# Weights fetched ahead in a handed-on area, gate stores on ScalarE's queue, and bfloat16 one-hots in pairs of tokens

## The reference

```python
mix = concat([mo * head_norm(mlstm), silu(rg) * head_norm(retention)])
x = x + mix @ w_out
hn = rmsnorm(x, rms_ffn_g)
# peer_ffn(hn): 8 heads, 128 x 128 experts, the best 16 for each token and head
q = hn @ w_query
s = einsum('thpd,hpkd->thpk', q, sub_keys)            # two halves p, 128 keys each
s1, i1 = top_k(s[:, :, 0], 16);  s2, i2 = top_k(s[:, :, 1], 16)
top_s, top_pos = top_k(s1[..., :, None] + s2[..., None, :], 16)   # over the 256 pairs
e_idx = (i1 * 128 + i2) at top_pos;  gate = softmax(top_s)
a = gelu(einsum('thkd,td->thk', peer_u[e_idx], hn))
x = x + einsum('thk,thkd->td', gate * a, peer_v[e_idx])
y = rmsnorm(x, rms_final_g)
```

## Time and profile before

| | us |
|---|---|
| median of 3 runs (3445.17 to 3450.38) | 3448.93 |
| the profiled execution | 3455.61 |
| its span | 3453.8 |
| load of a `wq`, 1 MB, from issue to landing (median) | 5.3 |
| store of a sub-block of the gate, 4 MB, from issue to landing (median) | 14.0 |
| mean granted clock of TensorE over the span, as a share of full speed | 0.969 |

### The profile page before, as it was taken

One profiled execution on the slowest core, in us unless ns is written; L12 is line 12 of the kernel. 1 busy time (PEld: TensorE's weight loads), 2 busy tenths in 40 slices (PEclk: granted clock), 3 DMA queues, 4 the chain that ended last, 5 costly groups with the idle time before them and its releaser, 6 DMA issues. The chain is left out here.

```text
span 3453.8 us, 49287 instructions
## 1 busy us (share of the span) xinstructions
PE 3288.0 (95%) x17444; PEld 2899.8 (84%) x17444; DVE 2489.7 (72%) x4965; ACT 991.0 (29%) x1479; POOL 737.1 (21%) x565
## 2 busy tenths in 40 slices
PE   7999999697999899999899999997999999999998
PEld 5766777486999899999899999986888888888886
DVE  5565545433999869999757777755888888988884
ACT  3212322221111123444322222222333334333332
POOL 0000000000000000000056656644333333433320
PEclk9999999798999999999999999998999999999999
DMA  2111110222111123556699999978999999999982
GB/s 103 38 38 50 52 49 26 74 80 86 68 68 68 54 86 114 180 180 209 193 349 373 373 364 359 362 296 311 403 367 352 353 353 371 380 369 352 354 318 110
DMA packets 323282, 749.94 MB, mean 217 GB/s; under 512 B 22312, under 2 KB 153772, under 8 KB 322016
## 3 DMA queue, kind: packets, MB, share of 16 engines
q1 hardware_dynamic: 243392, 458.51, 37.2%
q0 software_dynamic: 79776, 290.00, 22.3%
HBM read 633.48 MB, written 114.95 MB: 217 GB/s over the span
## 5 line engine op out<-in xcount | busy, mean ns | idle before, releaser
L1083 PE MATMUL u_p<-hn_hi,u_hi 128*128 128x384 f32 x2048 | 701.6, 343 | 35.9 <-PEq L1437 16.2
L1084 PE MATMUL u_p<-hn_lo,u_hi 128*128 128x384 f32 x2048 | 695.0, 339 | 0.0
L1085 PE MATMUL u_p<-hn_hi,u_lo 128*128 128x384 f32 x2048 | 694.8, 339 | 0.0
L1552 POOL DMA_INDIRECT s_ring<-in_peer_u,row_idx x264 | 332.1, 1258 | 1298.4 <-DVE row_idx L1642 1075.0
L1797 PE MATMUL y_p<-v_hi,w_hi 128*128 128x512 f32 x1536 | 474.5, 390 | 18.6 <-DVE w_lo L1882 17.0
L1754 POOL DMA_INDIRECT y_ring<-in_peer_v,row_idx x240 | 356.9, 1487 | 622.2 <-DVE yt L1891 555.9
L1802 PE MATMUL y_p<-v_hi,w_lo 128*128 128x512 f32 x1536 | 473.7, 390 | 0.0
L1799 PE MATMUL y_p<-v_lo,w_hi 128*128 128x512 f32 x1536 | 473.7, 390 | 0.0
L1823 ACT ACTIVATE v_hi<-v_raw 128x1024 fp32r<-128x1024 f32 x256 | 257.2, 1052 | 666.5 <-PE y_p L1802 654.5
L1878 DVE TENSOR_TENSOR v_lo<-v_raw,v_hi 128x1024 fp32r<-128x1024 f32 x256 | 302.1, 1221 | 171.1 <-ACT v_hi L1823 154.9
L1083 PEld LDWEIGHTS u_p<-hn_hi,u_hi 128*128 128x128 f32 x2048 | 387.9, 189 | 38.2 <-issue 24.8
(11 more groups left out here) (312 smaller groups left out, 4621.9 us busy)
## 6 DMA issues: line engine op xcount, KB each, us to landing
v_raw<-in_peer_v SPq DMA_DIRECT2D x128, 1024.0 KB
u_raw<-in_peer_ut SPq DMA_DIRECT2D x128, 512.0 KB
act_scratch<-act_tile SPq DMA_DIRECT2D x128, 384.0 KB
gate_scratch<-gbuf SPq DMA_DIRECT2D x12, 4096.0 KB, 14.0
a_raw<-act_scratch SPq DMA_DIRECT2D x128, 384.0 KB
g_raw<-gate_scratch SPq DMA_DIRECT2D x128, 384.0 KB, 8.7
wp_raw<-in_w_heads SPq DMA_DIRECT2D x64, 256.0 KB, 3.4
wq<-in_w_query SPq DMA_DIRECT2D x8, 1024.0 KB, 5.3
```

Source lines behind the costliest of these rows:

```text
L1083: mm(b, uh[:, s, k, :], hn_hi[:, k, t], start=(k == 0), stop=False)
L1084: mm(b, uh[:, s, k, :], hn_lo[:, k, t], start=False, stop=False)
L1085: last = mm(b, ul[:, s, k, :], hn_hi[:, k, t], start=False, stop=(k == ND - 1))
L1552: nc.gpsimd.indirect_dma_start(out=ring[:, s, :], out_offset=None, in_=src, in_offset=bass.IndirectOffsetOnAxis(ap=idx[:, column:column + ...
```

## The change

An area `late` of 32 KB a partition lives through the whole kernel and is handed from stage to stage: weights `wp_hi` and `wp_lo` of the heads, low parts of `w_out`, first query weights (raw, high, low) and `sub_keys`, work arrays of decode, second buffer of `gbuf`, `s_hb`, and two of the four slots of the down phase. With it:

1. `w_out` is loaded by SP after the last projection of the heads, all eight blocks at once, into the place of `xn_lo` (which is therefore in two parts, written by two operations). Five blocks are rounded within the block of the heads, the other three at the start of the output projection, and `out` takes the blocks in the order `WO`.
2. The first query weights and `sub_keys` are loaded after the last output product and rounded at the end of that block. The block that cleared semaphores is gone; GpSimd clears them in the blocks that follow.
3. The gate's store is issued on ScalarE's queue at the end of each sub-block, and the block's end waits for the first buffer only; GpSimd waits for the second ahead of the first load into `s_hb`.
4. The one-hots are bfloat16, with the two tokens of a pair innermost. The gate is split at the end of decode into three bfloat16 parts (`gp`), the keys are copied (`eb`), and a step has five VectorE operations (`one2` = second key, `raw` = first key, and `raw` times each gate part into `one1`) and 24 bfloat16 matmuls, which sum the three parts in PSUM; each reads one token of the pairs, every second element.
5. The first two slots of the down phase are loaded in the block before it, after the last dot product; the waits for the stores of the gelus move behind the other two loads.

The core of the diff, shortened:

```diff
+SLOT = 2 * D + 4 * TL * P
+class Query:                       # views into the area "late"
+        self.raw = late[:, 0:2048]...;  self.hi, self.lo = late_r[...] for n in (1, 2)
+        self.keys = late[:, 6144:8192]...
+class Pair:                        # one slot of the down phase: v, a, g in SLOT columns
+    def load(self, sp, A, a_dram, g_dram, g, j):    # the three loads of the old load()
+        late_r, late = twin(top, "late", [P, NK * SUB])
...
 mixer_stages, block of the heads:
+    wh, wl = (late[:, n * 4096:(n + 1) * 4096].rearrange("p (k d) -> p k d", k=ND) for n in range(2))
+    xla, wo_a = twin(own, "xn_lo_a", [P, 3, T]);   xlb, wo_b = twin(st, "xn_lo_b", [P, 5, T])
+WO = [3, 4, 5, 6, 7, 0, 1, 2]
+    def wo_high(act, j, wo_b=None):
+        raw, hi, lo = wo_parts(WO[j], wo_b)             # raw in xn_lo's place, hi in xn_hi's, lo in late
+        act.wait_ge(*wo_in[j])
+        nc.scalar.activation(hi, raw, ACT.Copy, scale=gnm[:, WO[j]:WO[j] + 1]).then_inc(wohi_done, 1)
+    def wo_low(dve, j, wo_b=None):
+        raw, hi, lo = wo_parts(WO[j], wo_b)
+        dve.wait_ge(wohi_done, j + 1)
+        nc.vector.scalar_tensor_tensor(lo, raw, gnm[:, WO[j]:WO[j] + 1], hi.bitcast(F32), ALU.mult,
+                                       ALU.subtract).then_inc(wolo_done, 1)
+            sp.wait_ge(S["pj_done"], NTILE)
+            for j, k in enumerate(WO):
+                sp.dma_start(wo_parts(k, wo_b)[0], A["w_out"][:, k, :]).then_inc(wo_in[j][0], 16)
...
+            for j in range(5):                          # ScalarE
+                wo_high(act, j, wo_b)
             head_root(NH - 1)
...
-                v.tensor_tensor(xl[:, :, s], pb..., xh[:, :, s].bitcast(F32), ALU.subtract).then_inc(S["lo"], 1)
+                v.tensor_tensor(xla[:, :, s], pk[:, 0:3, 0:r], xh[:, 0:3, s].bitcast(F32), ALU.subtract)
+                v.tensor_tensor(xlb[:, :, s], pk[:, 3:ND, 0:r], xh[:, 3:ND, s].bitcast(F32),
+                                ALU.subtract).then_inc(S["lo"], 1)
+                    if n == NTILE - 1:                  # VectorE
+                        wo_low(dve, 0, wo_b)
...
+            wo_low(dve, 1, wo_b)
             finish(NH - 1)
+            for j in range(2, 5):
+                wo_low(dve, j, wo_b)
 block of the output projection:
+            for s in old[0]:                            # GpSimd; expire() returns the old semaphores
+                pool.sem_clear(s)
-            for k in range(2):
-                sp.dma_start(wo[:, k, :], A["w_out"][:, k, :]).then_inc(wo_in[k], 16)
-            for k in range(2, ND):
-                sp.wait_ge(wolo_done, k - 1)
-                sp.dma_start(wo[:, k % 2, :], A["w_out"][:, k, :]).then_inc(wo_in[k % 2], 16)
+                if t == NT - 2:
+                    sp.wait_ge(y_done, 2 * NT)
+                    sp.dma_start(first_query.raw, A["w_query"][0]).then_inc(first_query.wq_in, 16)
+                    sp.dma_start(first_query.keys, A["sub_keys"]).then_inc(first_query.sk_in, 16)
-                    for k in range(ND):
+                    for j, k in enumerate(WO):
                         if u == 0:
-                            pe.wait_ge(wolo_done, k + 1)
+                            pe.wait_ge(wolo_done, j + 1)
+            act.wait_ge(first_query.wq_in, 16)
+            ac(first_query.hi, first_query.raw, ACT.Copy).then_inc(first_query.hi_done, 1)
             h_high(NT - 1)
...
             h_low(NT - 1)
+            dve.wait_ge(first_query.hi_done, 1)
+            v.tensor_tensor(first_query.lo, first_query.raw, first_query.hi.bitcast(F32), ALU.subtract)
 end of decode (VectorE):
+                dve.wait_ge(t_out, PET)
+                ch.mark(v.tensor_copy(e3s[:, :, :], e3T[:, :, DENSE:DENSE + NS]))
+                ch.mark(v.tensor_copy(eb[:, :, :], e3T[:, 0:2, 0:DENSE]))
+                ch.link(v.tensor_copy(gp[:, 0, :], e3T[:, 2, 0:DENSE]))
+                ch.link(v.tensor_tensor(left[:, :], e3T[:, 2, 0:DENSE], gp[:, 0, :], ALU.subtract))
+                ch.link(v.tensor_copy(gp[:, 1, :], left[:, :]))
+                ch.link(v.tensor_tensor(left[:, :], left[:, :], gp[:, 1, :], ALU.subtract))
+                ch.link(v.tensor_copy(gp[:, 2, :], left[:, :]))
 gate block:
+        one1 = sb(st, "one1", [P, 2, 3, TWO, NK, 2], BF16)
+        one2 = sb(st, "one2", [P, 2, TWO, NK, 2], BF16)
+        raw = sb(st, "raw", [P, TWO, NK, 2], BF16)
-                    sp.wait_ge(bank_out, (2 * NSTEP) * (2 * j + s + 1) + 4)
-                    sp.dma_start(g_dram[...], gbuf[:, s, ...]).then_inc(saved[s], 16)
-            for s in range(2):
-                sp.wait_ge(saved[s], 16 * (NSUB // 2) + 16)
+            sp.wait_ge(saved[0], 16 * (NSUB // 2) + 16)
-                            last = nc.tensor.matmul(pg[...], one2[:, b, k, :], one1[:, b, k, :], start=True, stop=True)
+                            for q in range(3):
+                                last = nc.tensor.matmul(pg[...], one2[:, b, k // 2, :, k % 2],
+                                                        one1[:, b, q, k // 2, :, k % 2], start=(q == 0), stop=(q == 2))
+                    act.wait_ge(bank_out, (2 * NSTEP) * (2 * j + s + 1) + 4)        # end of a sub-block
+                    nc.scalar.dma_start(g_dram[...], gbuf[s]...).then_inc(saved[s], 16)
-                        v.tensor_tensor(raw[:, :, :], io, col[1], ALU.is_equal).then_inc(raw_done, 1)
-                        v.tensor_tensor(one1[:, b], io, col[0], ALU.is_equal).then_inc(hot1, 1)
+                        v.tensor_tensor(one2[:, b], key, e2, ALU.is_equal).then_inc(hot2, 1)
+                        dve.wait_ge(hot1, 3 * i + 1)
+                        v.tensor_tensor(raw[:, :, :, :], key, e1, ALU.is_equal).then_inc(raw_done, 1)
                         dve.wait_ge(raw_done, i + 1)
-                        v.tensor_tensor(one2[:, b], raw[:, :, :], col[2], ALU.mult).then_inc(hot2, 1)
+                        for q in range(3):
+                            part = gp[:, q, t].rearrange(...).unsqueeze(2).broadcast_to(two)
+                            v.tensor_tensor(one1[:, b, q], raw[:, :, :, :], part, ALU.mult).then_inc(hot1, 1)
 block of the gathers:
+                if n == 15:                             # GpSimd
+                    pool.wait_ge(saved[1], 16 * (NSUB // 2) + 16)
+            sp.wait_ge(dot_done, NU)
+            for s in range(2):
+                Pair(sem, s, late[:, s * SLOT:(s + 1) * SLOT]).load(sp, A, a_dram, g_dram, 0, s)
             for p in range(2):
                 a_store(sp, NK - 2 + p, p)
-            for p in range(2):
-                sp.wait_ge(a_out[p], 16 * (NK // 2))
 down phase:
-            for s in range(SLOTS):
-                load(sp, 0, s, s)
+            for s in range(2, SLOTS):
+                slot[s].load(sp, A, a_dram, g_dram, 0, s)
+            for p in range(2):
+                sp.wait_ge(a_out[p], 16 * (NK // 2))
```

228 lines of the change are left out of this document (132 added, 96 removed).

## The result

| | us |
|---|---|
| before, median of 4 runs (3440.68 to 3450.38) | 3447.05 |
| changed, median of 4 runs (3359.57 to 3365.61) | 3363.03 |
| ratio, 95% interval | 0.9758 [0.9739, 0.9776] |
| the profiled execution of the changed kernel, its span | 3361.09, 3359.3 |
| a second set: before, median of 11; changed, median of 6 (3367.65 to 3377.53) | 3442.16; 3373.37 |

The two sets give 84 and 69 us less. The two profiled executions differ by more, 94.5 us of span. A ledger by stretches of TensorE's work says where; each border is a row of the timeline.

What follows compares the result with a forecast made beforehand. TensorE and VectorE were both taken as full in the gate stage, with TensorE standing at seams; gate steps -29.3 us and all else -41.7 summed to -71.0, from the median 3448.9 to 3378 us, range 3350 to 3430.

## What to carry to other kernels

Where two engines are full together, size the new work on both, and expect the stage to stop somewhat above the slower one, since they wait for each other in turn (2% here, 14.33 us for 14.08). The narrower type paid on VectorE only with a layout in which every operand has two neighbouring values innermost: the same data laid out otherwise turned a gain of 35 us in the stage into a loss of 212 (592.9 us from the first step to the end, against 381.2). At a seam between blocks, list everything that stands ahead of the next load in its queue and in the border, clears of semaphores too, and put work of the next stage into the stand that is left: two tiles moved into a stand of 12 us took it away.

## What the runs showed of the hardware that I had not expected

- TensorE's granted clock over the first 640 us lies between 0.93 and 0.96 from execution to execution of the same work, and moves a border by up to 19 us (630.37 to 649.15). Two profiled executions differ by this much without any change, so a ledger by stretches is read with a second profile beside it.
- An issue behind a 4 MB store on the same queue stands 10.7 to 12.7 us on SP, while the store's own issue takes 0.38 us; on ScalarE's queue, where nothing follows, the same store costs 0.38 us.
- Clearing a semaphore takes about 0.083 us of VectorE's time, an estimate from its idle time with 97 and with 20 of them (8.96 and 2.54 us), so 97 made a stand of 8 us in a block of their own.
- A bfloat16 matmul that reads every second element of both operands takes 0.057 us, against 0.056 with neighbouring ones.
